# Value projections of a split-precision transformer kernel: blocks of four contraction slices by 512 columns instead of eight by 256, and value stages half a block later

## The reference, cut to what matters

```python
qkv = h @ w_qkv                       # h: 256 x 1024, w_qkv: 1024 x 3072
q, k, v = jnp.split(qkv, ...)         # v: 256 x 1024 (512 columns in the block attention)
a = p[:, :, 0] - lam_full * p[:, :, 1]                      # differential attention, per head
o = jnp.einsum('bhqk,bkhe->bqhe', a, v)
o = rmsnorm(o, subln) * (1.0 - lambda_init)
x = x + o.reshape(B, S, D) @ w_o[layer]
```

## Time and profile before

| | |
|---|---|
| Median of three runs | 1755.77 us |
| Profiled execution, first to last instruction | 1753.6 us |
| TensorE matmuls | 1744.2 us, 99% of the span, 13030 instructions |
| VectorE | 1301.7 us, 74% |
| ScalarE | 1059.2 us, 60% |
| Value projection matmuls, 128x256 (three lines) | 912 of the 13030 |
| Mean DMA rate | 175 GB/s |

### The profile page before, as it was taken

The page is one execution under the profiler, slowest core; times in us unless marked ns, Lnnn a source line. Parts: engine busy times, 40 slices in busy tenths (PEclk is TensorE's granted clock), DMA queues, the critical chain, the costliest instruction groups (busy, mean ns, idle before and its releaser), DMA issues.

```text
span 1753.6 us, 33156 instructions
## 1 busy us (share of the span) xinstructions
PE 1744.2 (99%) x13030; PEld 1646.4 (94%) x13030; DVE 1301.7 (74%) x1899; ACT 1059.2 (60%) x1592; POOL 97.1 (6%) x144
## 2 busy tenths in 40 slices
PE   9999999999999999999999999999999999999998
PEld 8999999999999999999999999999999999998887
DVE  7668878877877886877876697788666876556665
ACT  6776566666666666666666766566454555346444
POOL 3000000122000013000000000003000020000000
PEclk9999999999999999999999999999999999999999
DMA  9445555534566544565554465655555544435652
GB/s 310 147 145 168 193 191 159 190 133 138 176 203 190 180 170 146 170 214 181 180 179 145 146 192 192 187 183 193 192 180 195 161 164 139 161 127 189 201 178 96
DMA packets 238483, 306.27 MB, mean 175 GB/s; under 512 B 13763, under 2 KB 212981, under 8 KB 238333
## 3 DMA queue, kind: packets, MB, share of 16 engines
q1 hardware_dynamic: 236708, 300.27, 52.5%
q0 software_dynamic: 1552, 4.28, 0.7%
q10 hardware_dynamic: 104, 0.07, 0.0%
HBM read 303.53 MB, written 1.07 MB: 174 GB/s over the span
## 4 chain that ended last, share of the span: by engine, by line
PE 99%; DVE 0%; ACT 0%; issue 0%; DVEq 0%; POOL 0%; POOLq 0%; ACTq 0%
PE ps L1111 22%; PE ps L1112 22%; PE ps L1113 22%; PE ps L1467 17%; PE ps L1469 9%; PE ps L1278 1%; PE ps L1298 1%; PE ps L1625 0%; PE ps L1124 0%; PE ps L1328 0%; PE ps L1315 0%; PE ps L1270 0%; PE ps L1395 0%; PE ps L1353 0%; PE ps L1386 0%; PE ps L1367 0%
## 5 line engine op out<-in xcount | busy, mean ns | idle before, releaser
L1683 DVE TENSOR_TENSOR sb_w_lo<-sb_raw,sb_w_hi 128x2048 fp32r<-128x2048 f32 x283 | 646.0, 2290 | 225.4 <-ACT sb_w_hi L907 224.6
L907 ACT ACTIVATE sb_w_hi<-sb_raw 128x2048 fp32r<-128x2048 f32 x283 | 538.5, 1908 | 160.5 <-PE ps L1113 78.7
L1111 PE MATMUL ps<-sb_a_hl,sb_w_hi 128*128 128x256 f32 x1840 | 529.3, 288 | 1.8 <-DVE sb_a_hl L1697 1.0
L1112 PE MATMUL ps<-sb_a_hl,sb_w_hi 128*128 128x256 f32 x1840 | 520.4, 283 | 0.0
L1113 PE MATMUL ps<-sb_a_hl,sb_w_lo 128*128 128x256 f32 x1840 | 520.2, 283 | 0.0
L1467 PE MATMUL ps<-sb_a_hl,sb_w_hi 128*128 128x512 f32 x1280 | 447.6, 393 | 0.0
L1111 PEld LDWEIGHTS ps<-sb_a_hl,sb_w_hi 128*128 128x128 f32 x1840 | 352.2, 191 | 9.8 <-issue 6.4
L1469 PE MATMUL ps<-sb_a_hl,sb_w_lo 128*128 128x256 f32 x1280 | 358.2, 280 | 0.0
L1112 PEld LDWEIGHTS ps<-sb_a_hl,sb_w_hi 128*128 128x128 f32 x1840 | 352.5, 192 | 0.4
L1113 PEld LDWEIGHTS ps<-sb_a_hl,sb_w_lo 128*128 128x128 f32 x1840 | 352.4, 192 | 0.0
L1467 PEld LDWEIGHTS ps<-sb_a_hl,sb_w_hi 128*128 128x128 f32 x1280 | 239.7, 187 | 53.2
(11 more groups left out here) (264 smaller groups left out, 1908.9 us busy)
## 6 DMA issues: line engine op xcount, KB each, us to landing
sb_raw<-in_ffn_w_up SPq DMA_DIRECT2D x102, 1024.0 KB, 5.3
sb_raw<-in_ffn_w_down SPq DMA_DIRECT2D x66, 1024.0 KB, 4.9
sb_raw<-in_da_w_qkv SPq DMA_DIRECT2D x23, 1024.0 KB, 5.2
sb_raw<-in_ffn_w_gate SPq DMA_DIRECT2D x22, 1024.0 KB, 5.3
sb_raw<-in_w_o SPq DMA_DIRECT2D x16, 1024.0 KB, 5.0
sb_raw<-in_sb_w_qkv SPq DMA_DIRECT2D x12, 1024.0 KB, 5.2
sb_raw<-in_xa_wkv SPq DMA_DIRECT2D x8, 1024.0 KB, 5.4
sb_raw<-in_w_in SPq DMA_DIRECT2D x8, 1024.0 KB, 5.4
```

The costliest lines, as they stand in the source:

```text
L907: act.activation(w_hi[:, a % RING, :], raw[:, a % RING, :], ACT.Copy).then_inc(hi_ready, 1)
L1111: pe.matmul(o, hi1, hi2, start=start, stop=False, skip_group_check=True)
L1112: pe.matmul(o, hi1, lo2, start=False, stop=False, skip_group_check=True)
L1683: dve.tensor_tensor(w_lo[:, a % RING, :], raw[:, a % RING, :], w_hi[:, a % RING, :].bitcast(F32), ALU.subtract).then_inc(lo_ready, 1)
```

## The change

Eighteen of the nineteen value blocks (all but that of sliding-window attention) are paired. A pair covers the same 512 columns; its first block holds contraction slices 0 to 3 of them, its second slices 4 to 7, so one block is four slices by 512 columns. Half j of each of the two blocks is still 128 tokens: four slices of three matmuls that move 512 columns. The two token halves accumulate in two banks of their own over both blocks. VectorE takes nothing out after the first block and both banks after the second (two instructions of 512 columns; `taken` rises by two). The value stages of differential attention move: `values` and `back` of groups 0 to 7 all one half later, with the left-out split kept at half 13. In stick-breaking attention `values` of groups 0 and 1 move one half later. The first `w_o` block walks the banks in another order in three of the mixers. In the bridge with `mv` blocks both wait for the same two banks.

```diff
 AT = {
     "diff": dict(scores=(5, 6, 9, 10, 17, 18, 21, 22), turn=(8, 9, 12, 13, 20, 21, 24, 25),
-                 values=(11, 12, 13, 14, 23, 24, 25, 26), back=(13, 14, 15, 16, 25, 26, 27, 28)),
+                 values=(12, 13, 14, 15, 24, 25, 26, 27), back=(14, 15, 16, 17, 26, 27, 28, 29), late=13),
     "stick": dict(scores=(5, 6, 9, 10, 17, 18, 21, 22), parts=(7, 8, 11, 12, 19, 20, 23, 24), suffix=(8, 9, 12, 13, 20, 21, 24, 25),
-                  values=(11, 12, 14, 15, 24, 25, 26, 27)),
+                  values=(12, 13, 14, 15, 24, 25, 26, 27)),
...
+        def paired(typ, form):
+            return typ == "mv" or typ == "v" and form != "slide"
+        def block_src(block, form):
+            typ, (w, l), c0, j = block
+            if paired(typ, form):
+                c0, r0 = c0 - j % 2 * BW, j % 2 * (D // 2)
+                return io[w][l][r0:r0 + D // 2, c0:c0 + 2 * BW].rearrange("(k p) n -> p k n", p=P)
+            return io[w][l][:, c0:c0 + BW].rearrange("(k p) n -> p k n", p=P)
...
-                late = at["back"][0] if form == "diff" else None
+                late = at["late"] if form == "diff" else None
...
+            def paired_product(acts, b, o, j, part, k):
+                wh, wl = weights(b, KC // 2)
+                c, js = part * (KC // 2) + k, slice(j * P, (j + 1) * P)
+                return product(o, a_hi[acts][:, c, js], a_lo[acts][:, c, js], wh[:, k, :], wl[:, k, :], c == 0, c == KC - 1)
...
-                    pe.wait_ge(u_free, u - 3)
+                    pe.wait_ge(u_free, u - 3 if typ == "mk" else ph["u"] - 2)
...
+                    if paired(typ, form):
+                        part = blk[3] % 2
+                        if j == 1 and part == 0:
+                            pe.wait_ge(taken, ph["tk"] + i - 1)
+                        for k in range(KC // 2):
+                            ins = paired_product(1 if typ == "mv" else 0, ph["n"] + i, PS[:, (i - part + j) % 3, :], j, part, k)
...
-                        order = [(k, m) for p in (2 * half, 2 * half + 1) for k in range(2) for m in (2 * p, 2 * p + 1)]
+                        banks = {"diff": ((0, 3), (1, 2)), "stick": ((0, 3), (1, 2)), "moba": ((2, 3), (0, 1))}
+                        order = [(k, m) for p in banks.get(form, ((0, 1), (2, 3)))[half] for k in range(2)
+                                 for m in (2 * p, 2 * p + 1)]
...
-                    pe.wait_ge(taken, taken_of(ph, ("v",), g // 2))
+                    pe.wait_ge(taken, taken_of(ph, ("v",), g // 4 * 2 + 1))
...
+            def take_values(j, banks, done):
+                es = slice((j - 1) * BW, (j + 1) * BW)
+                for q in range(QB):
+                    dve.tensor_scalar(v[:, q, es], banks[q], rT[:, q:q + 1], None, ALU.mult).then_inc(done, 1)
...
+                    if paired(typ, form) and j % 2 == 0:
+                        return
...
+                    if paired(typ, form):
+                        return take_values(j, [PS[:, (i - 1 + q) % 3, :] for q in range(QB)], taken)
...
-                    late = at["parts"][::2] if form == "stick" else at["back"][:1] if form == "diff" else ()
+                    late = at["parts"][::2] if form == "stick" else (at["late"],) if form == "diff" else ()
```

More of the change, by code:

```diff
@@ L421, in heads_of, with slices_of @@
             return [(keys[s * HD:(s + 1) * HD, g, :], slice((2 * g + s) * HD, (2 * g + s + 1) * HD)) for s in range(2)]
+        def paired(typ, form):
[6 more added lines that the diff above has]
+            return io[w][l][:, c0:c0 + BW].rearrange("(k p) n -> p k n", p=P)
+        def slices_of(block, form):
+            return KC // 2 if paired(block[0], form) else KC
         def arrival(form, c):
@@ L523, in _ @@
                 if ph["kind"] == "bridge":
-                    for i, (_, (w, l), c0, _) in enumerate(ph["blocks"]):
-                        src = io[w][l][:, c0:c0 + BW].rearrange("(k p) n -> p k n", p=P)
-                        load(ph["n"] + i, 0, slot(ph["n"] + i, KC), src)
+                    for i, blk in enumerate(ph["blocks"]):
+                        load(ph["n"] + i, 0, slot(ph["n"] + i, slices_of(blk, None)), block_src(blk, None))
                 elif ph["kind"] == "mix":
-                    for i, (_, (w, l), c0, _) in enumerate(ph["blocks"]):
+                    for i, blk in enumerate(ph["blocks"]):
                         if ph["n"] + i == RING:
                             small_loads()
-                        src = io[w][l][:, c0:c0 + BW].rearrange("(k p) n -> p k n", p=P)
+                        src = block_src(blk, ph["form"])
                         if ph["n"] + i == 0:
@@ L1146, in turn_root, with mem_product @@
                 ins.then_inc(rT_done, 1)
-            def mem_product(typ, b, o, j, k):
+            def mem_product(b, o, j, k):
                 wh, wl = weights(b, KC)
                 js, first, last = slice(j * P, (j + 1) * P), (j, k) == (0, 0), k == KC - 1
-                if typ == "mv":
-                    return product(o, a_hi[1][:, k, js], a_lo[1][:, k, js], wh[:, k, :], wl[:, k, :], first, last)
                 return product(o, wh[:, k, js], wl[:, k, js], a_hi[1][:, k, :], a_lo[1][:, k, :], first, last)
+            def paired_product(acts, b, o, j, part, k):
+                wh, wl = weights(b, KC // 2)
+                c, js = part * (KC // 2) + k, slice(j * P, (j + 1) * P)
+                return product(o, a_hi[acts][:, c, js], a_lo[acts][:, c, js], wh[:, k, :], wl[:, k, :], c == 0, c == KC - 1)
             def bridge(ph):
@@ L1170, in bridge @@
                     for j in range(2):
-                        for k in range(KC):
-                            ins = mem_product(typ, b, UB[u % 4][:, j * T:(j + 1) * T], j, k)
+                        for k in range(slices_of(ph["blocks"][i], None)):
+                            if typ == "mk":
+                                ins = mem_product(b, UB[u % 4][:, j * T:(j + 1) * T], j, k)
+                            else:
+                                ins = paired_product(1, b, UB[(ph["u"] + j) % 4], j, i % 2, k)
                             if (i, j, k) == ((1, 0, 3) if ph["mem_turned"] else (0, 1, 1)):
@@ L1805, in bridge @@
                         wait_root(ph["mem_turned"]["stat"])
-                    dve.wait_ge(blocks_done, ph["n"] + i + 1)
-                    mem_take(typ, j, UB[(ph["u"] + i) % 4], u_free)
+                    if typ == "mk":
+                        dve.wait_ge(blocks_done, ph["n"] + i + 1)
+                        dve.tensor_tensor(kT[:, 2 * j:2 * j + 2, :], pairs(UB[(ph["u"] + i) % 4]), both(r_all[:, 1, :]),
+                                          ALU.mult).then_inc(u_free, 1)
+                    elif i % 2:
+                        dve.wait_ge(blocks_done, ph["n"] + i + 1)
+                        take_values(j, [UB[(ph["u"] + q) % 4] for q in range(QB)], u_free)
             def final(ph):
```

17 lines of the change are left out of this document (7 added, 10 removed).

## The result

The changed kernel takes **1764.47 us** (median of five runs, 1763.25 to 1766.45), the kernel before 1755.77 (1755.73 to 1756.32). The ratio is 1.0049, with a 95% interval of 1.0039 to 1.0060: slower by about half a per cent, past the upper end of the predicted range (1764.0). The profiled execution went from a span of 1753.6 us to 1762.7, so 9.1 us are to be explained where the sum forecast 4.0.

What follows compares the result with a forecast made beforehand. TensorE's instruction stream, busy 99% of the span, was taken as the bound. The terms -3.6 - 0.2 + 6.2 + 1.6 = +4.0 us took 1755.8 to 1759.8 us, range 1753.4 to 1764.0.

Steps and rivals of the forecast that it cites:

- Halves: 36 paired value halves: 12 matmuls of 512 columns instead of 24 of 256 save 0.10 us each, 3.6 us.
- Rival A: Value halves: a 512-column matmul is cheaper than in the down block, 223 ns or less, down to 1751.7 us; chance 0.15.
- The interruption: `values(0)` moved to half 12, where other small matmuls stand: one interruption fewer in three mixers, 0.2 us saved.
- First place: `back(3)` at half 17, both differential mixers: TensorE waits 3.1 us each for `out_lo(2)` behind two splits, 6.2 us lost.
- B: Rival: the stall at `back(3)` is absent or short, giving 1753.6 us; chance 0.12.
- C: Rival: neither stall, at `back(3)` or the mixer's end, appears, giving 1752.0 us; chance 0.08.
- Second place: Mixer's end, `back(7)` at half 29: the last `w_o` block waits 0.8 us for `out_lo(6)`, 1.6 us for both mixers.
- Takes, loads, the stick-breaking list: VectorE's 512-column takes at 0.72 us and loads cost nothing; stick-breaking has about 0.3 us slack before its suffix matmuls.
- "No wait at ... bridge": Bridge: sum of squares reached 0.5 us later, but the first operands depending on it have over 1 us to spare.
- The forecast's own case: Both stalls and E, own range 1758 to 1762 us; chance 0.55.
- rival D: Each long stall lets the clock fall to 1.2 GHz, adding 2 us each: 1763.8 us; chance 0.10.
- E: Rival: tenths lost in differential mixers and stick-breaking, about 1761 us; chance within 0.55. In "E + 3.0": end of half 15.

Runs made afterwards that it cites:

- kernel 4: The kernel before, unpaired, with only the changed kernel's stage table (`values`, `back` one half later, left-out split kept at half 13): 1766.96 us, ratio 1.0065.
- experiment 7: Changed kernel with `back` at its old halves, plus the sum of squares in the `mv` bridge after 12 matmuls instead of 18: 1753.97 us.
- experiment 6: Changed kernel with 12 calls of unused identity matmuls in the wait ahead of `back(3)`: 1760.26 us; with 4 calls instead: 1763.54 us.
- experiment 1: Changed kernel with `back` of the differential mixers at its old halves (13 to 16, 25 to 28): 1754.83 us, ratio 0.9994.
- kernel 2: Changed kernel with `back` of groups 4 to 7 at old halves 25 to 28, groups 0 to 3 at the new 14 to 17: 1761.80 us.
- experiment 8: Changed kernel with `back` at its old halves, plus the second split of half 15 moved behind half 17's stages: 1753.25 us, ratio 0.9985.

## Why the prediction was wrong

The direction and the mechanism of both waits were right. The sum was not, 1759.8 forecast and 1764.47 measured, since it had the clock at nothing. By its steps:

- **Halves: held.** -3.6 forecast, 36 x 0.12 = -4.2 measured (230 ns a matmul for 232). Rival A, with 223 ns or less, did not come. The interruption was there in the two differential mixers (0.09 each: the half behind the old place of `values(0)` takes 2.87 us for 2.96) and not in stick-breaking, which the moved stages alone leave where it was (+0.02 in kernel 4). The formula that the prediction took from the Trainium skill ("TensorE: Matmul & The Clock Gate", section "Back-to-back issue gap") is given there for an isolated matmul, and the section says that a stream with weight loads is spaced otherwise; so 120 and 232 ns in this stream neither confirm nor refute it. Nothing in the sum hung on it.
- **First place: held.** 6.2 forecast, 6.3 measured; and each point of the chain within 0.05 us. With E at 69.56, ScalarE's splits start at E + 3.0, VectorE's at E + 4.96 (4.95 forecast), `out_lo(2)` at E + 9.37 (9.35), and TensorE goes on at E + 9.99 (10.0). Rivals B and C fell with it. Experiment 4 shows that the table alone makes it.
- **Second place: held.** 1.6 forecast, 1.6 measured.
- **Takes, loads, the stick-breaking list: held, all but a tenth.** 0.70 for 0.72 us, and no wait for a take or a load. The 0.3 us of slack before the suffix matmuls did not quite suffice: 0.11 and 0.04 us.
- **"No wait at ... bridge" failed.** The step followed the first operands behind the sum of squares, which have their 1 us, and left out that a weight split stands behind them in VectorE's list. It costs 0.8 to 0.9 us (ledger and experiment 7). Its own rule, that every instruction behind a delayed one has to be followed, was applied to `back` and not here.
- **The clock: this is the step that failed.** The forecast's own case took the wait at its length and let the clock stay full. It had rival D at a chance of 0.10, "each would add 2 us: 1763.8", and that is what came: 4.3 us by the windows, 4.2 by experiment 6. The kernel with the same late `back(3)` and next to no idle time takes 1760.26, within 0.5 us of the forecast; that it comes so near is in part luck, as the halves gained 0.6 us more than forecast and the bridge, the start, `values(7)` and the suffix matmuls cost 1.5 that it did not have. The working had no row with a wait of 3 us, and treated a missing row as a reason for the favourable case. Rival D's own price, 4 us for both, was right to 0.3; its chance was too low.

The terms as measured: -4.2 - 0.2 + 6.3 + 1.6 + 0.2 (`values(7)`) + 4.3 (clock) + 0.8 (bridge) + 0.36 (start) + 0.15 (suffix) = +9.3 us, against 9.1 between the two traces; the 0.2 is that of layer 3 in the ledger.

Of E only 0.08 in each of the two differential mixers came, at `values(7)`, and in stick-breaking the 0.15. What would have come in the place of the first wait, the 0.8 us at the scores, was no rival of the prediction; experiment 1 found it, once the wait ahead of it was gone.

What stays open: why the clock stays low for 3.4 us in one place and 6.8 in the other, behind waits of equal length and equal work. Kernels 2, 4 and the one with four filling calls had 3.4 in both, and there the clock fell 0.0 to 1.8 us after TensorE had gone on; the stretch of 6.8 is the only one that began before. The runs of the changed kernel differ by up to 3.2 us, those of the kernel with the wait filled by 1.0; the mean clocks of the slower ones are lower (0.995 with 1766.45; 0.997 and 0.998 with 1763.25 and 1763.79), which fits low stretches that vary in number or length from execution to execution, as in kernel 2, but their traces weren't taken. Whether the first wait could be had away while `back` stays at its new halves, by moving the second split as in experiment 8, was not run.

## What to carry to other kernels

Where one engine is busy 99% of the time, moving a stage by half a block is a change to every in-order list behind it: write out for each engine what stands ahead of the moved result and what stands behind the delayed one, down to the last consumer. A wait of 2 to 3 us on TensorE can cost more than its length, here two thirds as much again in the median (4.2 us on 6.3); count it with a price for the clock, or see to it that it doesn't arise. And when a wait is removed, look at once for the one that it was hiding, as putting `back` where it had been gave 1754.8 us here, and 1753.3 once the split behind it was moved too.

## What the runs showed of the hardware

- In the traces TensorE's clock fell from 2.4 to 1.2 GHz at idle times of 3.0 us and also of 2.0 us in the middle of a dense stream (eight places in four kernels), and stayed there for 3.4 us, once 6.8. It did so between 0.7 us before and 1.8 us after TensorE went on. By the mean clocks and times it did not fall in every execution: kernel 2 ranges from 1760.07 us at 0.999 to 1763.87 at 0.997. Behind waits up to 1.0 us (the kernel before, and experiment 1 with 0.8) no row shows it lower.
- Multiplications by the identity in place of the idle time (24 matmuls of 112 ns, 0.2 us left idle) kept the clock full: 0.999 or 1.000 in all nine executions.
- With a weight load ahead of each matmul, 512 moving columns are issued every 230 ns and 256 every 120 ns (value halves of 2.75 and 2.88 us): the larger one saves 10 ns in 240.
- VectorE takes 128x512 out of PSUM in 0.70 us (two in 1.41) where 128x256 took 0.48.
